# The embedding product of p_2 computed in the routing instead of in the feed-forward

## The chip, the cores and the metric

The kernel runs on one core of one Trainium2 chip. The metric is device time in microseconds (us) of one launch, as the median of several runs. The core has TensorE (PE, matmuls; PEld is its weight load), VectorE (DVE), ScalarE (ACT), GpSimd (POOL) and SyncE (SP, which only issues transfers here). Each engine works through a list of instructions of its own; the lists meet at semaphores.

## The reference

Two transformer blocks, one after the other, on x of 256 rows (tokens) by 1024 columns, all in float32. Cut to what matters here:

```python
# first block
x = x + concat([a_out, r_out]) @ w_out          # latent attention and retention
x = x + memory_cross_attention(rms_norm(x), rms_norm(mem), ...)
x = x + hierarchical_moe(rms_norm(x), ...)      # 4 groups of 8 experts: a router chooses for each token
                                                # one group, and two experts of that group
# second block
h = rmsnorm(x, g_mix);  z = h @ w_in            # recurrent and convolution heads
x = x + merged @ w_out
h = rmsnorm(x, g_ffn)
g, u = split(h @ w_gate_up)
x = x + (silu(g) * u) @ w_down                  # w_gate_up 1024 x 5632, w_down 2816 x 1024
gate = sigmoid(rmsnorm(x, g_ple) @ w_ple_gate)
x = x + gate * (p_i @ w_ple)                    # p_i = p_2, 256 x 256; w_ple 256 x 1024
return rmsnorm(x, g_final)
```

The product `p_i @ w_ple` depends on two inputs of the kernel alone, so it can be computed at any time before the last gate.

## The kernel before

Every float32 operand of a wide matmul is split in two parts of a shorter format: ACT copies the high part (names in `_hi`), DVE subtracts it from the source and keeps the low part (`_lo`), and PE adds three products (high by high, low by high, high by low: `three`, one line each in the profile, L2185 to L2187). Tokens lie in two tiles of 128 rows (t = 0, 1), columns in chunks of 512 (c = 0, 1); one matmul is 128 x 128 by 128 x 512 into one of eight PSUM banks.

Weights stream in units of 1 MB. SP loads unit u into one of three places of `stage` (in the expert part also into three places of `more`), ACT writes `w_hi` of it (L428 to L434), DVE `w_lo` (L441 to L449), PE uses it. `w_hi` and `w_lo` hold three units each: unit u takes the place of unit u - 3, so ACT waits for `unit_done` of that one, and SP's next load into a place of `stage` waits for `lo_ready`.

The order of the work is written out by hand, one list for each engine, in the places that the change touches as follows.

- **End of the cross attention.** PE multiplies by the four units of `cross_w_o` (`wide_unit` with U_CO to U_CO + 3). DVE in the meantime makes the low parts of the last units, runs a chain of tiny operations for the second block's decay (`lam_t`, `softplus2`, L1816 to L1827), the low part of the router's weights (`r_lo`), the low part of the first expert unit (U_MOE), and then `add_chunk(0, ...)`, L1739, which adds chunk 0 of the cross attention to x and signals `x_cross` = 1. After it come three constants (L1834 to L1836), the next unit and the low part of x. The second `add_chunk` signals `x_cross` = 2.
- **Routing.** PE transposes x for the router in two halves (`turn("moe", ...)`, L2190), the first on `x_cross` = 1, inside the last attention unit, the second on `x_cross` = 2. Then come 32 small products with the router's weights (L2506, L2508), the ranks of the tokens (L2515 to L2519) and, with DVE's `slot_of`, the gathering of the tokens for each expert (L2530, L2531). Between these stand 15 matmuls whose result nobody reads (`keep_busy`, L2490), 1 + 2 + 8 + 4.
- **Feed-forward of the second block.** 11 steps of 256 columns of the hidden layer. The columns of step 0 are computed first (`columns_of`, two units, 48 matmuls into banks 4 and 5); inside the second unit PE transposes p_2 (`turn_embed`); then `embed_product` computes `p_2 @ w_ple` with 24 matmuls into banks 0 to 3 from a weight unit of its own, U_PLE; ACT and DVE meanwhile turn step 0's columns into `hidden`. Then `turn_hidden(0)`, step 1 and so on. ACT copies the embedding product to `embed` (L1258).

Of the kernel before, what the change touches and what calls it, by code (L numbers as in the profile page):

```python
# [91 lines left out]
def program(nc, a, out, ctx):  # L92
# [78 lines left out]
    row_wide = xs[:, 1, 0:T * P].rearrange("p (t q) -> p t q", t=T)  # L171
    scale_row, scale_row2 = xs[:, 0, 0:256], xs[:, 0, 256:512]

# [65 lines left out]
    p_in = rb("p_in", [P, T, 256])  # L239
# [33 lines left out]
    embed, ple_gate = sb("embed", [P, T, D]), sb("ple_gate", [P, T, D])  # L273
# [35 lines left out]
    U_PLE = U_FFN + 2  # L309
    FFN_BASE = U_FFN + 1  # L310
# [7 lines left out]
    embed_unit = (a["w_ple_2"][0].rearrange("(p k) n -> p (k n)", k=2), 2048)  # L318
# [25 lines left out]
    main_pairs = swiglu_pairs(U_MOE, EXPERTS) | {U_FFN, FFN_BASE} | (swiglu_pairs(FFN_BASE, STEPS_FFN) - {FFN_BASE, FFN_BASE + 1})  # L344
# [35 lines left out]
    def slot_free(sp, st, u0):  # L380

        if st.last_in_slot(u0) is not None:
            sp.wait_ge(st.lo_ready, st.last_in_slot(u0) + 1)
        elif st is main and st.places[u0] >= RING:
            sp.wait_ge(sem("x_cross"), 1)

# [106 lines left out]
    def chunk_lo(dve, u0, c, st=main):  # L493
# [14 lines left out]
                + [f"mix{n}" for n in range(4)] + [("scales", 4)]  # L508
                + [("ffn0", 6), ("ffn1", 7), ("ffn2", 6), ("ffn3", 7), ("pT", 7), ("ple0", 4), ("ple1", 5), ("ple2", 6), ("ple3", 7)])
# [77 lines left out]

    def flat3(v):
        return v.rearrange("p k t -> p (k t)")
# [27 lines left out]
    def up_done(base, e):  # L617

        return base + 1 if isinstance(e, int) and e == 0 else e * 3 + (base + 1)
# [37 lines left out]

    def part_bank(k):

        return bank[k % 6]  # L660
# [126 lines left out]
    def _(sp):  # L787
# [16 lines left out]
        for u in range(3, U_MOE):  # L804
            load_unit(sp, *before[u], u)

        def swiglu_loads(both_of, down_of, base, steps, st=main, before_steps=None):
# [10 lines left out]
            if before_steps:  # L818
                before_steps(both)
            else:  # L820
                both(0, 0, base)
                both(0, 1, base + 1)
# [38 lines left out]
        def ffn_start(both):  # L861
            both(0, 0, U_FFN)
            both(0, 1, U_FFN + 1)
            load_unit(sp, *embed_unit, U_PLE)

        swiglu_loads(lambda c, half: [gu2[:, 4 * half:4 * half + 4, w, bass.ds(c * FF, FF)] for w in range(2)],
                     lambda c: down2[bass.ds(c, 1)].rearrange("c p n -> p (c n)"), FFN_BASE, STEPS_FFN,
                     before_steps=ffn_start)
# [11 lines left out]
    def _(pool):  # L880
# [10 lines left out]
        pool.wait_ge(sem("rx_hi"), 1)  # L891
# [6 lines left out]
    def _(act):  # L898
# [334 lines left out]
        warm_up(ACT.Exp)  # L1233
        act.wait_ge(sem("route_diffs"), 1)
        nc.scalar.activation(exps[:], diffs[:], ACT.Exp).then_inc(sem("route_exps"), 1)

        def swiglu(name, base, steps, scale_of):

            def tanhs(e):
                act.wait_ge(unit_done, up_done(base, e))  # L1240
                for t in range(T):
                    nc.scalar.activation(silu_t[:, t], bank[4 + t][:, 0:FF], ACT.Tanh, scale=scale_of(t)).then_inc(sem(name + "_tanh"), 1)
# [5 lines left out]
            def step(i, first=False):  # L1248
                if not first:
                    split_hi(act, SLOT, base + 1, 3, i)  # L1250
# [19 lines left out]
        def experts(name, st, base, groups, nth_tail, before_tail=None, splits=(None, None)):  # L1270

            for k in range(KD):
                act.wait_ge(sem(name + "_gathered"), k + 1)
# [4 lines left out]
                ins.then_inc(sem(name + "_xg_hi"), 1)  # L1278
# [1683 lines left out]
```

## Time and profile before

| | us |
|---|---|
| median of 3 runs | 960.63 |
| lowest and highest run | 958.66, 961.14 |
| span of the profiled execution, first to last instruction | 957.2 |
| PE busy in it | 941.8 (98%) |
| DVE busy | 743.1 (78%) |
| ACT busy | 621.3 (65%) |
| SP's transfers, share of 16 DMA engines | 63.2% |

The profiled execution has no time of its own beside its span; the median lies 3.43 us above the span, for what runs ahead of the first and behind the last instruction. A busy time of PE counts matmuls whose ends are modelled and overlap, so the starts of the matmuls, not their lengths, tell the pace. "Busy" does not tell either what PE does: the 15 matmuls of `keep_busy` count in it.

### The profile page before, as it was taken

The page shows a single profiled execution, that of the slowest core. Times are in us where ns is not written, and L with a number is a line of the kernel's source. Part 1 is how long each engine was busy: PE and PEld are TensorE (multiplying, and loading weights), DVE is VectorE, ACT ScalarE, POOL GpSimd, SP SyncE. Part 2 cuts the span into 40 slices and gives each one's busy share as a digit, 9 for nine tenths or more (in the row PEclk, how much of TensorE's full clock was granted, in tenths as well). Part 3 has the DMA queues.
Part 4 walks back from the last instruction along what each step waited for, and adds up shares of the span by engine and source line. Part 5 has one row for each costly group of instructions (what it writes and reads, how often), then busy time and mean ns, then how long its engine had stood idle before and what let it go on. Part 6 is the DMA issues. An engine that isn't in the chain of part 4 may idle for free.

```text
span 957.2 us, 13873 instructions
## 1 busy us (share of the span) xinstructions
PE 941.8 (98%) x5047; PEld 811.6 (85%) x5047; DVE 743.1 (78%) x1105; ACT 621.3 (65%) x946; POOL 20.5 (2%) x40
## 2 busy tenths in 40 slices
PE   8999999999999999999999999999999999999996
PEld 7888888888888888888888899999998888888885
DVE  6657696658799999999999889888896655555575
ACT  6785784665678878788787675757564644434455
POOL 2400000000000000000000000000000000000000
PEclk9999999999999999999999999999999999999998
DMA  9855336416299999999997364736465656555521
GB/s 340 239 182 180 132 94 214 164 58 250 95 372 372 343 367 369 355 365 370 358 372 271 111 225 126 255 120 210 152 234 183 220 179 204 186 177 182 199 102 44
DMA packets 102668, 214.68 MB, mean 224 GB/s; under 512 B 5644, under 2 KB 60192, under 8 KB 96992
## 3 DMA queue, kind: packets, MB, share of 16 engines
q1 hardware_dynamic: 100928, 211.57, 63.2%
q0 software_dynamic: 1392, 2.20, 0.9%
q8 instruction: 26, 0.43, 0.2%
q10 hardware_dynamic: 304, 0.33, 0.1%
q14 instruction: 18, 0.15, 0.0%
HBM read 213.03 MB, written 1.05 MB: 224 GB/s over the span
## 4 chain that ended last, share of the span: by engine, by line
PE 91%; DVE 4%; ACT 3%; issue 1%; DMA 1%; SPq 0%; DVEq 0%; ACTq 0%
PE bank L2185 22%; PE bank L2187 22%; PE bank L2186 22%; PE bank L2848 5%; PE bank L2849 5%; PE bank L2850 5%; PE bank L2190 4%; PE bank L2455 1%; DMA xs<-in_mem_dram 1%; DVE w_lo L449 1%; PE bank L2530 0%; PE bank L2531 0%; PE bank L2875 0%; PE bank L2876 0%; PE bank L2874 0%
## 5 line engine op out<-in xcount | busy, mean ns | idle before, releaser
L2185 PE MATMUL bank<-w_hi,xT_hi 128*128 128x512 f32 (+1 forms) x704 | 279.8, 397 | 0.6 <-DVE xT_lo L1522 0.3
L2187 PE MATMUL bank<-w_hi,xT_lo 128*128 128x512 f32 (+1 forms) x704 | 274.3, 390 | 0.0
L2186 PE MATMUL bank<-w_lo,xT_hi 128*128 128x512 f32 (+1 forms) x704 | 274.0, 389 | 0.0
L2185 PEld LDWEIGHTS bank<-w_hi,xT_hi 128*128 128x128 f32 x704 | 132.7, 189 | 27.3 <-issue 2.1
L2187 PEld LDWEIGHTS bank<-w_hi,xT_lo 128*128 128x128 f32 x704 | 132.1, 188 | 27.5
L2186 PEld LDWEIGHTS bank<-w_lo,xT_hi 128*128 128x128 f32 x704 | 132.4, 188 | 25.1
L447 DVE TENSOR_TENSOR w_lo<-stage,w_hi 128x1024 fp32r<-128x1024 f32 (+3 forms) x98 | 112.3, 1146 | 30.8 <-ACT w_hi L433 29.5
L2848 PE MATMUL bank<-xT_hi,w_hi 128*128 128x256 f32 x440 | 124.8, 284 | 0.4 <-DVE w_lo L449 0.4
L2849 PE MATMUL bank<-xT_lo,w_hi 128*128 128x256 f32 x440 | 124.5, 283 | 0.0
L2850 PE MATMUL bank<-xT_hi,w_lo 128*128 128x256 f32 x440 | 124.5, 283 | 0.0
L433 ACT ACTIVATE w_hi<-stage 128x1024 fp32r<-128x1024 f32 (+3 forms) x99 | 98.5, 995 | 31.8 <-PE bank L2187 14.5
L449 DVE TENSOR_TENSOR w_lo<-stage,w_hi 128x1024 fp32r<-128x1024 f32 (+3 forms) x98 | 111.9, 1142 | 0.0
L434 ACT ACTIVATE w_hi<-stage 128x1024 fp32r<-128x1024 f32 (+3 forms) x99 | 97.8, 988 | 0.0
L441 DVE TENSOR_TENSOR w_lo<-stage,w_hi 128x1024 fp32r<-128x1024 f32 x55 | 67.1, 1220 | 28.5 <-ACT w_hi L428 27.8
L428 ACT ACTIVATE w_hi<-stage 128x1024 fp32r<-128x1024 f32 x55 | 58.3, 1059 | 44.0 <-PE bank L2187 44.0
L2848 PEld LDWEIGHTS bank<-xT_hi,w_hi 128*128 128x128 f32 x440 | 84.4, 192 | 0.7 <-DVE w_lo L449 0.6
L2850 PEld LDWEIGHTS bank<-xT_hi,w_lo 128*128 128x128 f32 x440 | 84.4, 192 | 0.0
L2849 PEld LDWEIGHTS bank<-xT_lo,w_hi 128*128 128x128 f32 x440 | 84.4, 192 | 0.0
L2185 PE MATMUL bank<-w_hi,aT_hi 128*128 128x512 f32 x212 | 82.7, 390 | 0.1
L2187 PE MATMUL bank<-w_hi,aT_lo 128*128 128x512 f32 x212 | 82.8, 390 | 0.0
L2186 PE MATMUL bank<-w_lo,aT_hi 128*128 128x512 f32 x212 | 82.5, 389 | 0.0
L443 DVE TENSOR_TENSOR w_lo<-stage,w_hi 128x1024 fp32r<-128x1024 f32 x55 | 67.0, 1217 | 0.0
(425 smaller groups left out, 1384.0 us busy)
## 6 DMA issues: line engine op xcount, KB each, us to landing
stage<-in_w_in_dram SPq DMA_DIRECT2D x36, 1024.0 KB, 5.1
stage<-in_w_gate_up_dram SPq DMA_DIRECT2D x44, 512.0 KB, 4.6
more<-in_expert_w_down_dram SPq DMA_DIRECT2D x17, 1024.0 KB, 6.2
stage<-in_expert_w_gate_dram SPq DMA_DIRECT2D x33, 512.0 KB, 5.1
stage<-in_expert_w_up_dram SPq DMA_DIRECT2D x33, 512.0 KB, 6.3
more<-in_expert_w_gate_dram SPq DMA_DIRECT2D x31, 512.0 KB, 5.1
more<-in_expert_w_up_dram SPq DMA_DIRECT2D x31, 512.0 KB, 6.0
stage<-in_expert_w_down_dram SPq DMA_DIRECT2D x15, 1024.0 KB, 6.8
```

The costliest lines, as they stand in the source:

```text
L433: nc.scalar.activation(w_hi[:, s, 0:half], src[:, 0:half], ACT.Copy).then_inc(st.half_ready, 1)
L434: nc.scalar.activation(w_hi[:, s, half:cols], src[:, half:cols], ACT.Copy).then_inc(st.hi_ready, 1)
L441: nc.vector.tensor_tensor(beside(w_lo, s, 0), of_both(st, u0, 0), beside(w_hi, s, 0).bitcast(F32), ALU.subtract)
L443: nc.vector.tensor_tensor(beside(w_lo, s, 1), of_both(st, u0, 1), beside(w_hi, s, 1).bitcast(F32), ALU.subtract).then_inc(st.lo_ready, 1)
L447: nc.vector.tensor_tensor(w_lo[:, s, 0:half], src[:, 0:half], w_hi[:, s, 0:half].bitcast(F32), ALU.subtract)
L449: nc.vector.tensor_tensor(w_lo[:, s, half:cols], src[:, half:cols], w_hi[:, s, half:cols].bitcast(F32), ALU.subtract).then_inc(st.lo_ready, 1)
L2185: mm(o, k_hi, v_hi, start=start, stop=False)
L2186: mm(o, k_hi, v_lo, start=False, stop=False)
L2187: return mm(o, k_lo, v_hi, start=False, stop=stop)
L2848: mm(o, w_hi[:, s, at:at + P], xT_hi[:, k, :], start=k == 0, stop=False)
L2849: mm(o, w_hi[:, s, at:at + P], xT_lo[:, k, :], start=False, stop=False)
L2850: ins = mm(o, w_lo[:, s, at:at + P], xT_hi[:, k, :], start=False, stop=k == KD - 1)
```

## The change

`p_2 @ w_ple` moves from the feed-forward into the end of the cross attention and the routing.

- Weights and input: `w_ple` is loaded by SP behind the load of U_CO, into memory of its own (`ple_in`), and split by ACT (`ple_hi`) and DVE (`ple_lo`) there. The unit U_PLE is gone, so the feed-forward's units are numbered on without it. p_2 is loaded early, into `hidden`.
- PE transposes p_2 inside unit U_CO + 2 (before its second of four slices). ACT and DVE split the transposed tile (`aT_hi`, `aT_lo`) right behind the splitting of U_CO + 3.
- The 15 unread matmuls are gone. In their places stand the 24 matmuls of the product: 9 before the second half of the router's transposes, 9 behind the router's products, 6 behind the ranks. The router's 32 products now stand in one piece.
- ACT copies the product to `embed` before the routing's exponentials; `embed` takes the memory of `xs`, so results that nobody reads of the later squares go elsewhere.
- The gathering uses the banks in the order 4, 5, 2, 3, 0, 1 and waits for the copies of the embedding product in banks 2, 3, 0, 1.
- Feed-forward: step 0's columns go to banks 2 and 3, step 1's to 4 and 5, so both are computed back to back, and `turn_hidden(0)` stands between the two units of step 1.
- SP's first load into `more` also waits for `ple_lo`. The expert part and its second pass for overflowing groups, which is not run with this input, share semaphores.

```diff
@@ SP
         for u in range(3, U_MOE):
             load_unit(sp, *before[u], u)
+            if u == U_CO:
+                sp.wait_ge(sem("x_attn"), 1)
+                sp.dma_start(ple_in[:], a["w_ple_2"][0].rearrange("(p k) n -> p (k n)", k=2)).then_inc(sem("ple_loaded"), 16)
...
-            load_unit(sp, *embed_unit, U_PLE)
@@ ACT
         nc.scalar.activation(r_hi[:], r_w[:], ACT.Copy).then_inc(sem("router_hi"), 1)
+        act.wait_ge(sem("ple_loaded"), 16)
+        act.wait_ge(unit_done, U_CO + 1)
+        for n in range(2):
+            at = slice(1024 * n, 1024 * n + 1024)
+            nc.scalar.activation(ple_hi[:, at], ple_in[:, at], ACT.Copy).then_inc(sem("ple_hi"), 1)
         splits_to(U_CO + 4)
+        copy_to(aT_hi[:], "pT").then_inc(sem("pT_hi"), 1)
         warm_up(ACT.Sqrt)
         splits_to(U_MOE + 2)
...
         warm_up(ACT.Exp)
+        for n, (c, t) in enumerate(EMBED_ORDER):
+            act.wait_ge(sem("embed_filled"), n + 1)
+            nc.scalar.activation(embed[:, t, 512 * c:512 * c + 512], bank[2 * c + t][:, :], ACT.Copy).then_inc(sem("embed_copied"), 1)
         act.wait_ge(sem("route_diffs"), 1)
...
-                if first:
-                    for c in range(2):
-                        for t in range(T):
-                            nc.scalar.activation(embed[:, t, 512 * c:512 * c + 512], bank[2 * c + t][:, :],
-                                                 ACT.Copy).then_inc(sem("embed_copied"), 1)
@@ DVE
         low_parts("catc", None, (2, 3))
+        splits_to(U_CO + 3)
+        for n in range(2):
+            at = slice(1024 * n, 1024 * n + 1024)
+            dve.wait_ge(sem("ple_hi"), n + 1)
+            ins = tt(ple_lo[:, at], ple_in[:, at], ple_hi[:, at].bitcast(F32), ALU.subtract)
+        ins.then_inc(sem("ple_lo"), 1)
         splits_to(U_CO + 4)
+        dve.wait_ge(sem("pT_hi"), 1)
+        frees(tt(flat3(aT_lo[:]), bank[where["pT"][0]][:, :], flat3(aT_hi[:]).bitcast(F32), ALU.subtract), "pT")
@@ PE
-        wide_unit(U_CO + 2, C_CO, 1, 512, xT_hi, xT_lo, "catc")
+        wide_unit(U_CO + 2, C_CO, 1, 512, xT_hi, xT_lo, "catc", before={1: turn_embed})
...
-        for half in range(2):
-            if half == 0:
-                b = to_fill(pe, "router")
...
-                if k == 2:
-                    turn("moe", x, [("x_cross", 2)], (2, 3))
-                if k % 4 == 0:
-                    keep_busy(1 + half)
...
+        been_read(pe, "pT")
+        pe.wait_ge(sem("ple_lo"), 1)
+        embed_product([(0, 0), (0, 1), (1, 0)])
+        turn("moe", x, [("x_cross", 2)], (2, 3))
+        b = to_fill(pe, "router")
...
-        keep_busy(8)
+        embed_product([(1, 1), (2, 0), (2, 1)])
         pe.wait_ge(sem("group_chosen"), 1)
...
-        keep_busy(4)
+        embed_product([(3, 0), (3, 1)])
...
                 for k in range(6):
+                    if t == 0 and k >= 2:
+                        pe.wait_ge(sem("embed_copied"), k - 1)
                     ins = gather(k, t)
...
             columns_of(0, U_FFN, 0, 0, before={2: lambda: turn("ffn", x, [("x_rnn", 2)], (2, 3))})
-            columns_of(1, U_FFN + 1, 0, 0, before={3: turn_embed})
-            embed_product()
-            turn_hidden(0)
+            columns_of(1, U_FFN + 1, 0, 0)
...
-                pe.wait_ge(sem(name + "_hidden"), i * 2)
+                if not first:
+                    pe.wait_ge(sem(name + "_hidden"), i * 2)
                 columns_of(0, base - 1, 3, i)
+                if first:
+                    turn_hidden(0)
                 columns_of(1, base, 3, i)
@@ new functions on PE
+        def embed_product(blocks):
+            for n, k in blocks:
+                c, t = EMBED_ORDER[n]
+                at = D * k + 512 * c
+                ins = three(bank[2 * c + t][:, :], aT_hi[:, k, P * t:P * t + P], aT_lo[:, k, P * t:P * t + P],
+                            ple_hi[:, at:at + 512], ple_lo[:, at:at + 512], start=k == 0, stop=k == 1)
+                if k == 1:
+                    ins.then_inc(sem("embed_filled"), 1)
+    EMBED_ORDER = ((1, 0), (1, 1), (0, 0), (0, 1))
+    def columns_bank(e, t):
+        return bank[(2 if isinstance(e, int) and e == 0 else 4) + t]
```

DVE at the end of the cross attention, from the low parts of U_CO + 3 to the addition that signals `x_cross` = 1 (`w_lo<-stage` is the splitting of a weight unit, `ple_lo` that of w_ple, `lam_t` the first link of the chain of tiny operations, `r_parts` the router's weights), before:

```order
L1530 TENSOR_TENSOR xT_lo<-bank,xT_hi 128x512 x2
L447 TENSOR_TENSOR w_lo<-stage,w_hi 128x1024
L449 TENSOR_TENSOR w_lo<-stage,w_hi 128x1024
L1816 TENSOR_SCALAR lam_t<-lam_t 128x8
...
L1827 TENSOR_SCALAR lam_t<-softplus 128x8
L1829 TENSOR_TENSOR r_parts<-r_w,r_parts 128x8x36
...
L441 TENSOR_TENSOR w_lo<-stage,w_hi 128x4x256
L443 TENSOR_TENSOR w_lo<-stage,w_hi 128x4x256
L1739 TENSOR_TENSOR x<-x,bank 128x512 x2
```

and now:

```order
L1539 TENSOR_TENSOR xT_lo<-bank,xT_hi 128x512 x2
L1825 TENSOR_TENSOR ple_lo<-ple_in,ple_hi 128x1024 x2
L451 TENSOR_TENSOR w_lo<-stage,w_hi 128x1024
L453 TENSOR_TENSOR w_lo<-stage,w_hi 128x1024
L1829 TENSOR_TENSOR aT_lo<-bank,aT_hi 128x512
L1833 TENSOR_SCALAR lam_t<-lam_t 128x8
...
L1844 TENSOR_SCALAR lam_t<-softplus 128x8
L1846 TENSOR_TENSOR r_parts<-r_w,r_parts 128x8x36
...
L445 TENSOR_TENSOR w_lo<-stage,w_hi 128x4x256
L447 TENSOR_TENSOR w_lo<-stage,w_hi 128x4x256
L1748 TENSOR_TENSOR x<-x,bank 128x512 x2
```

Two splittings of w_ple stand ahead of U_CO + 3, and the splitting of the transposed p_2 (`aT_lo`) ahead of the chain; what follows is in the order that it had.

PE from the last transposes of x in the attention to the gathering (`r_parts` 128x72 and 128x36 are the router's products, 16 in each half before, `hot` the ranks, `slot_of` the gathering), before:

```order
L2190 MATMUL bank<-const,x 128x128 x8
...
L2495 MATMUL bank<-zeros,before_it 128x144
L2490 MATMUL bank<-r_parts,before_it 128x512
L2506 MATMUL bank<-r_parts,xT_hi 128x72
L2508 MATMUL bank<-r_parts,xT_lo 128x36
...
L2190 MATMUL bank<-const,x 128x128 x8
...
L2490 MATMUL bank<-r_parts,before_it 128x512 x2
...
L2490 MATMUL bank<-r_parts,before_it 128x512 x8
L2515 MATMUL bank<-hot,before_it 128x4
...
L2490 MATMUL bank<-r_parts,before_it 128x512 x4
L2530 MATMUL bank<-slot_of,xs_hi 128x512
```

and now:

```order
L2206 MATMUL bank<-const,x 128x128 x8
...
L2201 MATMUL bank<-ple_hi,aT_hi 128x512
L2202 MATMUL bank<-ple_lo,aT_hi 128x512
L2203 MATMUL bank<-ple_hi,aT_lo 128x512
...
L2206 MATMUL bank<-const,x 128x128 x8
L2527 MATMUL bank<-zeros,before_it 128x144
L2534 MATMUL bank<-r_parts,xT_hi 128x72
L2536 MATMUL bank<-r_parts,xT_lo 128x36
...
L2543 MATMUL bank<-hot,before_it 128x4
...
L2557 MATMUL bank<-slot_of,xs_hi 128x512
```

The unread products with `before_it` and `r_parts` of 512 columns are gone; the first of the triplets with `ple_hi` stand ahead of the second transposes of x (9 matmuls), further ones between the router's products and the ranks (9) and between the ranks and the gathering (6).

PE at the start of the feed-forward (`p_in` is p_2, `xT_hi` are columns of a step, `aT_hi` with `w_hi` the embedding product), before:

```order
L2187 MATMUL bank<-w_hi,xT_lo 128x512
L2190 MATMUL bank<-const,p_in 128x128 x4
L2185 MATMUL bank<-w_hi,xT_hi 128x512
...
L2185 MATMUL bank<-w_hi,aT_hi 128x512
...
L2190 MATMUL bank<-const,hidden 128x128 x4
L2185 MATMUL bank<-w_hi,xT_hi 128x512
```

and now:

```order
L2203 MATMUL bank<-w_hi,xT_lo 128x512
L2206 MATMUL bank<-const,hidden 128x128 x4
L2201 MATMUL bank<-w_hi,xT_hi 128x512
L2202 MATMUL bank<-w_lo,xT_hi 128x512
L2203 MATMUL bank<-w_hi,xT_lo 128x512
```

The columns of step 0 and the first unit of step 1 run on into each other, and the transposes of `hidden` follow on these.

## Rows read from the trace of the kernel before

**Rows 1.** The page: engine busy times, and the chain that ended last by engine.

```profile
PE 941.8 (98%) x5047; PEld 811.6 (85%) x5047; DVE 743.1 (78%) x1105; ACT 621.3 (65%) x946; POOL 20.5 (2%) x40
...
PE 91%; DVE 4%; ACT 3%; issue 1%; DMA 1%; SPq 0%; DVEq 0%; ACTq 0%
```

**Rows 2.** Chain that ended last, in order, 215 to 256: start us, us, what.

```profile
223.46 1.28 DVE x L1739 x2
...
230.15 1.20 DVE x L1739 x2
...
239.97 0.61 PE bank L2530
```

**Rows 3.** Timeline of DVE: start us, us, instruction, count, idle time before and releaser.

```profile
213.73 1.23 DVE L447 TENSOR_TENSOR w_lo<-stage,w_hi 128x1024 fp32r<-128x1024 f32 x1 [1.04 <-ACT w_hi L433]
...
216.01 0.17 DVE L1816 TENSOR_SCALAR lam_t<-lam_t 128x8 f32<-128x8 f32 x1
...
220.19 1.23 DVE L441 TENSOR_TENSOR w_lo<-stage,w_hi 128x1024 fp32r<-128x1024 f32 x1
...
223.46 1.28 DVE L1739 TENSOR_TENSOR x<-x,bank 128x512 f32<-128x512 f32 x2 [0.91 <-PE bank L2187]
...
224.66 0.22 DVE L1834 TENSOR_SCALAR ones<-const 128x128 fp32r<-128x128 f32 x1
```

**Rows 4.** Timeline of ACT, end of the cross attention.

```profile
212.64 1.06 ACT L433 ACTIVATE w_hi<-stage 128x1024 fp32r<-128x1024 f32 x1
```

**Rows 5.** Timeline of PE, end of the cross attention and routing.

```profile
217.82 0.39 PE L2185 MATMUL bank<-w_hi,xT_hi 128*128 128x512 f32 x1
...
227.34 1.03 PE L2190 MATMUL bank<-const,x 128*128 128x128 f32 x8
...
231.40 1.09 PE L2190 MATMUL bank<-const,x 128*128 128x128 f32 x8
...
235.77 2.09 PE L2490 MATMUL bank<-r_parts,before_it 128*128 128x512 f32 x8
...
239.97 0.61 PE L2530 MATMUL bank<-slot_of,xs_hi 128*128 128x512 f32 x1 [0.17 <-issue]
...
246.22 0.63 PE L2530 MATMUL bank<-slot_of,xs_hi 128*128 128x512 f32 x1
```

**Rows 6.** Windows: stretch, us, busy us of PE, PEld, DVE, ACT, POOL, clock, DMA, GB/s.

```profile
170.00:212.00 42.00, 41.56 (x211) 35.21 (x210) 24.12 (x47) 25.69 (x56) 0.00 (x0) 1.00 0.37 125
...
223.46:229.60 6.14, 6.14 (x33) 5.14 (x31) 6.10 (x12) 5.24 (x10) 0.00 (x0) 1.00 0.54 185
...
229.60:239.97 10.37, 9.68 (x63) 7.65 (x61) 8.66 (x28) 5.12 (x11) 0.00 (x0) 1.00 0.99 390
...
239.97:252.85 12.88, 12.87 (x61) 12.03 (x61) 9.97 (x52) 6.17 (x17) 0.00 (x0) 1.00 0.02 6
...
950.50:951.00 0.50, 0.00 (x0) 0.00 (x0) 0.47 (x2) 0.46 (x3) 0.00 (x0) 0.70 0.00 0
```

**Rows 7.** Timeline of PE, start of the feed-forward.

```profile
742.10 0.63 PE L2190 MATMUL bank<-const,p_in 128*128 128x128 f32 x4
...
744.21 0.50 PE L2185 MATMUL bank<-w_hi,aT_hi 128*128 128x512 f32 x1
...
749.81 0.63 PE L2190 MATMUL bank<-const,hidden 128*128 128x128 f32 x4
```

**Rows 8.** Timeline of ACT and DVE, start of the feed-forward.

```profile
742.76 0.60 ACT L975 ACTIVATE aT_hi<-bank 128x512 fp32r<-128x512 f32 x1 [2.61 <-PE bank L2190]
...
743.46 0.69 DVE L2124 TENSOR_TENSOR aT_lo<-bank,aT_hi 128x512 fp32r<-128x512 f32 x1 [1.79 <-ACT aT_hi L975]
...
745.27 1.28 ACT L1242 ACT_TABLE_LOAD   x1
...
747.08 0.79 DVE L1873 SCALAR_TENSOR_TENSOR silu_g<-silu_t,bank 128x256 f32<-128x256 f32 x2 [0.37 <-ACT silu_t L1242]
...
750.97 1.57 ACT L1258 ACTIVATE embed<-bank 128x512 f32<-128x512 f32 x3
```

More of the change, by code:

```diff
@@ L270, in program @@
     expert_memory.close()
-    embed, ple_gate = sb("embed", [P, T, D]), sb("ple_gate", [P, T, D])
+    routing_memory = ExitStack()
+    routing_memory.enter_context(nc.sbuf_tensor("before_embed", [P, 5120], F32))
+    ple_hi, ple_lo = (routing_memory.enter_context(nc.sbuf_tensor(n, [P, SLOT], F32R)) for n in ("ple_hi", "ple_lo"))
+    routing_memory.enter_context(nc.sbuf_tensor("between_embed", [P, 896], F32))
+    ple_in = routing_memory.enter_context(nc.sbuf_tensor("ple_in", [P, SLOT], F32))
+    routing_memory.close()
+    embed, p_in = xs, hidden
+    ple_gate = sb("ple_gate", [P, T, D])
     fin_g = sb("fin_g", [P, D])
@@ L816, in step @@
                 load_unit(sp, down_of(i), 2048, base + n + 4, st=st)
[L818 to L822, printed above, removed]
+            both(0, 0, base)
+            both(0, 1, base + 1)
             for i in range(steps - 1):
@@ L2116, in _ @@
         add_chunk(1, C_OUT2, U_OUT2 + 3, "x_rnn")
-        stats(x, xs, [("x_rnn", 2)], "ffn")
+        stats(x, ple_gate, [("x_rnn", 2)], "ffn")
         low_parts("ffn", FFN_G, (2, 3))
         halves("ffn")
-        splits_to(U_PLE + 1)
         dve.wait_ge(sem("norm_half"), NORMS.index("ffn") + 1)
         then(tt(ffn_scale[:], half_rstd[:], rstd[:], ALU.mult))
-        dve.wait_ge(sem("pT_hi"), 1)
-        frees(tt(flat3(aT_lo[:]), bank[where["pT"][0]][:, :], flat3(aT_hi[:]).bitcast(F32), ALU.subtract), "pT")
         swiglu("ffn", FFN_BASE, STEPS_FFN, lambda t, e: ffn_scale[:, t:t + 1])
@@ L2412, in _, with turn_embed @@
         wide_unit(U_CQ + 2, C_CQ, 1, 512, xT_hi, xT_lo, "crossq")
+        def turn_embed():
+            pe.wait_ge(sem("last_loaded"), 16)
+            b = to_fill(pe, "pT")
+            view = p_in[:].rearrange("p t (q k) -> p t k q", k=2)
+            for k in range(2):
+                for t in range(T):
+                    ins = transpose(b[:, 256 * k + P * t:256 * k + P * t + P], view[:, t, k])
+            fills(ins, "pT")
+        def embed_product(blocks):
[6 more added lines that the diff above has]
+                    ins.then_inc(sem("embed_filled"), 1)
         def turn_queries(p):
@@ L2897, in _ @@
                           last=(lambda: turn("ffn", x, [("x_rnn", 1)], (0, 1))) if half and c else None)
-        def turn_embed():
-            pe.wait_ge(sem("last_loaded"), 32)
-            b = to_fill(pe, "pT")
-            view = p_in[:].rearrange("p t (q k) -> p t k q", k=2)
-            for k in range(2):
-                for t in range(T):
-                    ins = transpose(b[:, 256 * k + P * t:256 * k + P * t + P], view[:, t, k])
-            fills(ins, "pT")
-        def embed_product():
-            been_read(pe, "pT")
-            pe.wait_ge(lo_ready, U_PLE + 1)
-            s = U_PLE % RING
-            for c in range(2):
-                for k in range(2):
-                    for t in range(T):
-                        at = D * k + 512 * c
-                        ins = three(bank[2 * c + t][:, :], aT_hi[:, k, P * t:P * t + P], aT_lo[:, k, P * t:P * t + P],
-                                    w_hi[:, s, at:at + 512], w_lo[:, s, at:at + 512], start=k == 0, stop=k == 1)
-            ins.then_inc(unit_done, 1)
         swiglu("ffn", FFN_BASE, STEPS_FFN)
```

164 lines of the change are left out of this document (76 added, 88 removed), and 2 rows, old and new, of the table products.

## The prediction

> **What bounds the kernel now.** I read the page first: PE is busy 98% of the span and 91% of the chain that ended last is PE's [rows 1]. So a matmul taken off PE is worth its time, unless another engine decides at that place. The places where the change works are two, and I read each for itself.
>
> In the feed-forward PE starts a matmul every 0.23 us without a pause, so it is the bound there. The embedding product runs from 744.21 to 749.81 [rows 7].
>
> In the routing the busy share misleads, because 15 matmuls there are read by nobody. The view to read is the chain in order of time: at 223.46 it is on DVE (the addition of chunk 0 to x), at 230.15 again (the addition of chunk 1), and for the gathering it is back on PE at 239.97 [rows 2]. DVE is busy 6.10 of the 6.14 us from 223.46 to 229.60, where PE leaves the attention [rows 6], and the only idle time that it had shortly before is 0.91 us in front of the addition at 223.46, waiting for PE [rows 3]. So whatever comes to DVE before 223.46 beyond 0.91 us moves the routing.
>
> **The feed-forward: what PE saves.** Removed are the four transposes of p_2, which start at 742.10, and the product. The matmuls' pace: from 217.82, the start of a unit, to 227.34 stand 24 + 18 = 42 matmuls [rows 5], 9.52 / 42 = 0.227 us each. Six matmuls follow the transposes in their unit, and the product starts at 744.21. So transposes, six matmuls and the wait for the split p_2 take 744.21 - 742.10 = 2.11 us, of which the six matmuls are 1.36; 0.75 goes. Of that about 0.46 are the transposes and 0.25 the wait. The product is 749.81 - 744.21 = 5.60 us [rows 7]. Together 6.35 us.
>
> What is late next is step 1. Its first unit needs no result of step 0 and can follow at once: its splitting now stands where U_PLE's stood, ahead of 742. `turn_hidden(0)` needs `hidden`, which DVE has some 3 us after the end of step 0's columns (before: end of the columns at 744.0, then `aT_hi` and a unit's copy on ACT, table load at 745.27, DVE's gating at 747.08 [rows 8]); the 24 matmuls in between give 5.4 us of cover. The second unit of step 1 must be split behind the tanh: ACT's table load can start at 743.6 instead of 745.27, so DVE's gating comes at about 745.4 and the low part 3.9 us later, at 749.3; PE wants it at 743.5 + 5.45 + 0.4 = 749.35. I charge 0.1 us; the end of 0.6 us holds if ACT and DVE each lose 0.25 more. The embedding copies on ACT, some 0.5 us each (three of them in 1.57 us [rows 8]), leave this place and hid nothing. The loads are one less. Feed-forward: -6.25 us, between -6.35 and -5.75.
>
> **The end of the cross attention: what DVE gets.** Everything here is of forms that the trace shows.
>
> PE: the four transposes of p_2 stand behind six matmuls of unit U_CO + 2, which starts at 217.82: 217.82 + 6 x 0.227 = 219.18. They cost PE 0.46 us as before.
>
> ACT: the two copies of w_ple come first, at 212.64 where the unit U_CO + 3 was copied [rows 4], which moves to about 214.6 to 216.6. Then ACT waits for the transposes. Before, ACT's `aT_hi` started 0.66 us and DVE's `aT_lo` 1.36 us behind the start of the transposes (742.10, 742.76, 743.46), and DVE was free about 0.61 us later [rows 7, 8]. So `aT_hi` at 219.84, `aT_lo` at 220.54, DVE free at 221.15. Behind `aT_hi` ACT has a table load, 1.28 us as in [rows 8], and U_MOE's copy, from 221.85 on.
>
> DVE: at 213.73 stands the low part of U_CO + 3, two instructions 1.14 us apart, then the chain from 216.01 [rows 3]. Now `ple_lo` takes 213.73 to 216.01, U_CO + 3 to 218.29, and then DVE waits 2.25 us for `aT_hi`. Queued behind the waiting instruction are the chain of tiny operations (216.01 to 220.19, 4.18 us), U_MOE (220.19 to 222.47) and the addition at 223.46 that PE's transposes wait for [rows 3]. From 221.15 they end at 227.61. The addition is late by 227.61 - 223.46 = 4.15 us: 2.28 of `ple_lo`, 0.61 of `aT_lo`, 2.25 of waiting, less 0.99 of slack (the 0.91 and what lies between).
>
> All of this is passed on. PE reaches the transposes at 227.34 + 0.46 = 227.80 and waits 1.1 us for `x_cross` = 1. DVE goes on late by 4.15 without slack to the second addition, at 234.30. PE has then finished the unit and the first 9 matmuls of the product by about 233.4 and waits some 2.2 us. PE's 0.46 us and these 9 matmuls are free in this.
>
> The Trainium skill, "TensorE: Matmul & The Clock Gate", section on the array's architecture, says that ACT and DVE take their instructions in strict order, only PE pulling weight loads ahead; this speaks against putting a wait in front of the chain. The trace agrees: the constant `ones` needs nothing that is late, yet DVE idled 0.91 us at 223.46 with it queued and did it at 224.66 [rows 3]. Could DVE pass the waiting instruction, the chain would fill the 2.25 us and the sum would come out at -4.1 us instead of -1.9.
>
> **The routing itself.** Before, the second transposes start at 231.40, directly on `x_cross` = 2, and the gathering at 239.97, 8.57 us later [rows 5]. Now: the router's 32 products stand in one piece behind them; that costs about 0.2 us, since the first 16 no longer run before. The 9 product matmuls behind (2.04 us) replace the 8 unread ones that start at 235.77 and last 2.09 us, to 237.86 [rows 5]; that was just ahead of the ranks, so this is covered to 0.1 us. The 6 behind the ranks replace 4: 2 x 0.227 = 0.45 more, of which about 0.2 was idle (0.17 before 239.97). So the gathering starts later by 0.35 us beside the 4.15. DVE allowed its seventh pair only at 246.22 [rows 5], about 0.15 us after PE could have gone on, so 0.2 stays. The copies to `embed` on ACT, 0.5 each, end ahead of the last bank's turn, which comes 2.5 us into the gathering. I take +0.2 us; the ends are 0 and 0.8 (nothing hidden: 0.2 + 0.45 + a wait on the last copy). The load of w_ple is one unit among SP's others at a place where the queues are 37% busy (170 to 212 [rows 6]), 40 us ahead of its use; zero. `more` is loaded 4.2 us later with the rest, and the queues were at 2% from 239.97 to 252.85 [rows 6], so the experts do not wait: zero, at most 0.3.
>
> **Sum.** -6.25 + 4.15 + 0.2 = -1.9 us. The span goes from 957.2 to 955.3, and with the 3.43 us between span and median the median goes from 960.63 to **958.7 us**. The addition's 4.15 is uncertain by 0.7 either way (start of the transposes, semaphore times); with the bounds above the case's own range is 957.5 to 960.1.
>
> **Rivals.**
>
> *The lateness is absorbed.* Then only PE's own part counts: -6.25 + 0.46 + 0.2 = -5.6, 955.0 us. It needs DVE's wait for `aT_hi` and the `ple_lo` work to lie in slack that I did not see, for example an addition that is not what the routing turns on. Against it stands the chain, which has DVE without a gap there [rows 2], and DVE's busy time of 6.10 in 6.14 us [rows 6]. Half of it (2 us of lateness less) gives 956.8. Chance 0.16 for both.
>
> *The clock falls.* The only place of the trace where the granted clock fell, from 1.00 to 0.50 with 0.70 as the mean of the half microsecond between (950.50 to 951.00 [rows 6]), is about 2.3 us behind the last matmul, which ended at 948.36. The new pauses are 1.1 and 2.2 us, and the second is followed by transposes and matmuls of 36 to 72 columns until about 240, where 1 + 2 full ones stood before. If the clock goes to 1.2 GHz there, a full matmul costs twice 0.227: 15 of the product's add 3.4 us, behind which DVE's ranks and the gathering wait, and about 7 gathering matmuls 1.7 more. +5.1 us: 963.8 us, slower than now. It is slower than now from 1.9 us on, that is, from 8 full matmuls at the low level; against it speaks that the pause is a little shorter than the one at the end, and that the clock held at 1.00 through 229.60 to 239.97 with 0.7 us idle and many small matmuls [rows 6]. Chance 0.20.
>
> *The change doesn't shorten the feed-forward.* If step 1's second unit came late by the whole splitting (2.3 us) instead of 0.1, the sum would be +0.3, 960.9 us. ACT starting 1.7 us earlier speaks against it. It counts as part of "no change", chance 0.04.
>
> **Numbers.** Forecast 0.60, absorbed 0.16, clock 0.20, late unit 0.04. A difference of 0.3% is 2.9 us, about what a measurement of this kernel tells from no change; it lies at 957.7 and 963.5. Faster: the absorbed cases 0.14 of 0.16 and the forecast's lower tail, 0.08: 0.22. Slower: most of the clock's case and a bit else: 0.18. The same: 0.60. The range for 8 in 10 leaves out about half of each rival: 955.4 to 963.5 us.
>
> **What the profile would show.** DVE's addition to x after U_CO + 2 at about 227.6 instead of 223.46, with an idle time of 2.2 us in front of `aT_lo`; two waits of PE for the additions, 1.1 and 2.2 us; the gathering at 244.3; in the feed-forward the matmuls of step 0 and of step 1's first unit without a gap, `turn_hidden(0)` 5.4 us behind the end of step 0's columns, and no triplets with `aT_hi` between them; granted clock 1.00 through the routing. Wrong would be: an addition at 225 or earlier, no pause of PE before the second transposes, a clock under 1.00 in the routing, or a wait of PE for `w_lo` at the second unit of step 1.

## The result, and the profile after

The changed kernel takes 962.86 us (median of 5 runs, 959.74 to 964.21), the kernel before, beside it, 959.66 us (5 runs, 958.66 to 961.14). The ratio is 1.0029 with the interval [1.0019, 1.0040]: slower by some 2.8 us (the medians differ by 3.2), where 1.9 us less was forecast. The profiled execution took 962.86 us with a span of 961.1 us, 3.9 us more than the 957.2 of before.

The page after, in the lines that answer to [rows 1]:

```profile
PE 943.4 (98%) x5032; PEld 813.8 (85%) x5032; DVE 743.3 (77%) x1105; ACT 621.6 (65%) x946; POOL 20.5 (2%) x40
...
PE 91%; DVE 5%; ACT 2%; issue 1%; DMA 1%; SPq 0%; DVEq 0%; ACTq 0%
```

PE has 15 matmuls less (the unread ones; the product and its transposes have only moved) and is yet busy for 1.6 us longer. A busy time that grows with fewer instructions says that some of them became slower.

DVE's timeline after, against [rows 3] (start, us, instruction, idle time before and releaser):

```profile
220.37 0.69 DVE L1829 TENSOR_TENSOR aT_lo<-bank,aT_hi 128x512 fp32r<-128x512 f32 x1 [2.12 <-ACT aT_hi L979]
...
227.44 1.28 DVE L1748 TENSOR_TENSOR x<-x,bank 128x512 f32<-128x512 f32 x2
...
234.05 1.28 DVE L1748 TENSOR_TENSOR x<-x,bank 128x512 f32<-128x512 f32 x2
...
242.26 0.23 DVE L711 COPY biased<-bank 128x72 f32<-128x72 f32 x1 [3.11 <-PE bank L2536]
...
247.07 0.17 DVE L724 SCALAR_TENSOR_TENSOR hot_rank<-bank,hot 128x8 f32<-128x8 f32 x1 [2.26 <-PE bank L2547]
```

Down to the second addition this is the forecast: the wait for `aT_hi`, the addition at 227.44 instead of 223.46. The last two rows are not. DVE waits 3.11 us for the router's products and 2.26 us for the ranks, both PE's; the bound of this stretch has passed from DVE to PE.

PE's timeline after, against [rows 5]:

```profile
228.77 1.09 PE L2206 MATMUL bank<-const,x 128*128 128x128 f32 x8 [0.88 <-DVE x L1748]
...
232.97 0.40 PE L2203 MATMUL bank<-ple_hi,aT_lo 128*128 128x512 f32 x1
235.38 1.09 PE L2206 MATMUL bank<-const,x 128*128 128x128 f32 x8 [2.01 <-DVE x L1748]
...
241.77 0.38 PE L2536 MATMUL bank<-r_parts,xT_lo 128*128 128x36 f32 x1
241.99 0.77 PE L2201 MATMUL bank<-ple_hi,aT_hi 128*128 128x512 f32 x1
242.56 0.63 PE L2202 MATMUL bank<-ple_lo,aT_hi 128*128 128x512 f32 x1
242.99 0.63 PE L2203 MATMUL bank<-ple_hi,aT_lo 128*128 128x512 f32 x1
...
246.89 0.77 PE L2201 MATMUL bank<-ple_hi,aT_hi 128*128 128x512 f32 x1
...
249.60 0.63 PE L2557 MATMUL bank<-slot_of,xs_hi 128*128 128x512 f32 x1
```

The pauses of 0.88 and 2.01 us are the forecast's 1.1 and 2.2. But the product's matmuls start 0.43 us apart (242.56, 242.99), where the full matmuls of the kernel before stood 0.227 us apart at 217.82 to 227.34. Windows of the changed kernel, against [rows 6] (stretch, us, busy us of PE, PEld, DVE, ACT, POOL, granted clock, DMA, GB/s):

```profile
237.00:237.50 0.50, 0.50 (x7) 0.50 (x6) 0.49 (x2) 0.50 (x2) 0.00 (x0) 1.00 0.86 295
237.50:238.00 0.50, 0.50 (x6) 0.50 (x5) 0.50 (x2) 0.14 (x1) 0.00 (x0) 0.64 0.93 246
238.00:250.50 12.50, 12.50 (x43) 10.88 (x43) 6.64 (x27) 5.23 (x9) 0.00 (x0) 0.50 0.49 193
...
251.00:251.50 0.50, 0.50 (x3) 0.41 (x2) 0.45 (x2) 0.22 (x1) 0.00 (x0) 0.70 0.00 0
251.50:253.00 1.50, 1.50 (x8) 1.50 (x8) 1.26 (x8) 0.00 (x0) 0.00 (x0) 1.00 0.04 11
```

The granted clock is the share of TensorE's full 2.4 GHz that it ran at. From about 237.6 to 251.2 us it stands at 0.50, the level of 1.2 GHz, though PE is busy without a gap. Ahead of the fall lie the 2.01 us of waiting, eight transposes and some ten products of 36 and 72 columns.

The feed-forward, against [rows 7 and 8], two rows of the kernel before first:

```profile
729.03 1.03 PE L2190 MATMUL bank<-const,x 128*128 128x128 f32 x8
...
766.64 0.63 PE L2190 MATMUL bank<-const,hidden 128*128 128x128 f32 x4
```

and after:

```profile
738.86 1.03 PE L2206 MATMUL bank<-const,x 128*128 128x128 f32 x8
...
758.72 0.63 PE L2206 MATMUL bank<-const,hidden 128*128 128x128 f32 x4
...
770.11 0.63 PE L2206 MATMUL bank<-const,hidden 128*128 128x128 f32 x4
```

The turn of x that ends the recurrent block starts 9.8 us later than before (729.03), but the turn of step 1's `hidden` only 3.5 us later (before 766.64): 31.25 us lie between the two instead of 37.61, so 6.36 us are saved. With 0.4 us that the last stage is longer this is the whole difference of the two spans: 9.83 - 6.36 + 0.4 = 3.9 us.

### The profile page after: what moved, and what is told of

The parts are those of the page before. It is cut to its first block, busy times and chain, and to the rows that moved or that the text cites. A ratio compares the mean times of both kernels' runs of the same rounds, so it can differ in the third digit from the quotient of the medians.

```text
span 961.1 us, 13854 instructions
## 1 busy us (share of the span) xinstructions
PE 943.4 (98%) x5032; PEld 813.8 (85%) x5032; DVE 743.3 (77%) x1105; ACT 621.6 (65%) x946; POOL 20.5 (2%) x40
## 4 chain that ended last, share of the span: by engine, by line
PE 91%; DVE 5%; ACT 2%; issue 1%; DMA 1%; SPq 0%; DVEq 0%; ACTq 0%
PE bank L2201 22%; PE bank L2203 22%; PE bank L2202 22%; PE bank L2876 5%; PE bank L2877 5%; PE bank L2878 5%; PE bank L2206 4%; PE bank L2490 1%; DMA xs<-in_mem_dram 1%; DVE w_lo L453 0%; PE bank L2558 0%; PE bank L2557 0%; DVE w_lo L445 0%; PE bank L2903 0%; PE bank L2904 0%
## 5 line engine op out<-in xcount | busy, mean ns | idle before, releaser
L451 DVE TENSOR_TENSOR w_lo<-stage,w_hi 128x1024 fp32r<-128x1024 f32 (+3 forms) x97 | 111.1, 1145 | 27.3 <-ACT w_hi L437 26.1
L437 ACT ACTIVATE w_hi<-stage 128x1024 fp32r<-128x1024 f32 (+3 forms) x98 | 97.4, 994 | 32.5 <-PE bank L2203 14.5
L453 DVE TENSOR_TENSOR w_lo<-stage,w_hi 128x1024 fp32r<-128x1024 f32 (+3 forms) x97 | 110.8, 1142 | 0.0
L438 ACT ACTIVATE w_hi<-stage 128x1024 fp32r<-128x1024 f32 (+3 forms) x98 | 96.8, 988 | 0.0
L2203 PE MATMUL bank<-w_hi,aT_lo 128*128 128x512 f32 x204 | 79.6, 390 | 0.0
L2201 PE MATMUL bank<-w_hi,aT_hi 128*128 128x512 f32 x204 | 79.5, 389 | 0.0
L2202 PE MATMUL bank<-w_lo,aT_hi 128*128 128x512 f32 x204 | 79.4, 389 | 0.0
```

Source lines behind the costliest of these rows:

```text
L437: nc.scalar.activation(w_hi[:, s, 0:half], src[:, 0:half], ACT.Copy).then_inc(st.half_ready, 1)
L438: nc.scalar.activation(w_hi[:, s, half:cols], src[:, half:cols], ACT.Copy).then_inc(st.hi_ready, 1)
L451: nc.vector.tensor_tensor(w_lo[:, s, 0:half], src[:, 0:half], w_hi[:, s, 0:half].bitcast(F32), ALU.subtract)
L453: nc.vector.tensor_tensor(w_lo[:, s, half:cols], src[:, half:cols], w_hi[:, s, half:cols].bitcast(F32), ALU.subtract).then_inc(st.lo_ready, 1)
L2201: mm(o, k_hi, v_hi, start=start, stop=False)
L2202: mm(o, k_hi, v_lo, start=False, stop=False)
```

## The experiments

Theory 1 is that the lost clock turned the small gain into a loss. Theory 2 is that DVE's lateness and the new order did. Twelve kernels ran in three groups of four, each group beside the kernel before (959.1 to 959.3 us). A mean clock is the granted clock averaged over a whole run; the kernel before has 0.995 to 0.998. Some code lines are shortened.

**1. Unread matmuls in PE's second pause.**

```diff
         embed_product([(0, 0), (0, 1), (1, 0)])
+        for _ in range(8):
+            mm(bank[6][:, :], before_it[:], r_parts 512 columns, start=True, stop=True)
         turn("moe", x, [("x_cross", 2)], (2, 3))
```

> The changed kernel with eight unread 128x512 matmuls (8 x 0.227 = 1.82 us at the full clock) put into TensorE's wait of 2.01 us in front of the transposes at 235.4 us. Theory 1, the lost clock is what made the change slower: the granted clock stays at 1.00 from 236 to 251 us, the router's pitch is 0.107 instead of 0.213 us, the MoE's first columns start some 5 us earlier than in the changed kernel (near 253 instead of 258 us), and the time is about 0.998 of the kernel before (957.5 to 958.5 us). Theory 2, VectorE's late addition and the new order cost the time and the clock only goes along with it: the clock may stay up, but VectorE's and ScalarE's chain ends where it ended, and the time stays within 1 us of the changed kernel's, 1.002 to 1.004 of before. Theory 3, the clock isn't kept by matmuls in that pause (it falls for what is in the router's small products): the granted clock is 0.50 from about 238 us all the same, and the time is 1.003 of before or a little over it.

Measured: 958.35 us, ratio 0.9996 [0.9985, 1.0007], 12 runs: the median is 0.8 us under that of the kernel before, where the changed kernel's was 3.2 us over it. The interval takes in no difference, so this is a loss undone, not a gain. The nine runs with a mean clock of 0.995 or more have a median of 957.7 us. The profiled run had a span of 956.1 us. Its windows (PE alone: stretch, us, busy us, granted clock, DMA, GB/s), then DVE's first addition and PE's timeline:

```profile
232.00:235.00 3.00, 3.00 (x14) 1.00 0.80 284
235.00:238.00 3.00, 2.85 (x25) 1.00 0.99 348
238.00:241.00 3.00, 3.00 (x25) 1.00 1.02 365
```

```profile
227.61 1.28 DVE L1748 TENSOR_TENSOR x<-x,bank 128x512 f32<-128x512 f32 x2
...
235.55 1.09 PE L2206 MATMUL bank<-const,x 128*128 128x128 f32 x8 [0.15 <-DVE x L1748]
...
239.97 0.26 PE L2538 MATMUL bank<-r_parts,xT_lo 128*128 128x36 f32 x1
240.09 0.48 PE L2201 MATMUL bank<-ple_hi,aT_hi 128*128 128x512 f32 x1
...
244.42 0.46 PE L2559 MATMUL bank<-slot_of,xs_hi 128*128 128x512 f32 x1
```

DVE's second addition stands where it stood (234.22; 234.05 in the changed kernel), and with the clock at 1.00 the gathering starts at 244.42 instead of 249.60; the forecast had 244.3. Theory 1 holds, and theory 2 falls: DVE's lateness is still there, and the loss is gone. Not every run kept the clock: the eight at 957.1 to 958.9 us have a mean clock of 0.995 to 0.998 and the one at 959.2 us has 0.996, but the one at 960.1 us has 0.994, and the two at 961.6 and 962.2 us have 0.993.

**2. The kernel before without its unread matmuls** (`keep_busy` issues none).

> The kernel before with its 15 unread matmuls in the routing left out, nothing else. It prices the clock without the change's other parts. Theory 1: the granted clock falls to 0.50 in the routing, somewhere in 230 to 240 us, the gathering starts and ends 3 to 5 us later, and the time is 1.003 to 1.005 of before (962.5 to 964.5 us). Theory 2: within 0.1% of before, since the routing is set by VectorE's and ScalarE's chain, and the gathering alone pays for a lower clock (under 1 us).

Measured: 961.5 us, ratio 1.0028 [1.0017, 1.0039], the mean clock 0.991 to 0.993 in all 7 runs. The router's pitch doubles at 234.3 us, without any pause over 0.67 us before it:

```profile
232.00:234.00 2.00, 1.33 (x14) 1.00 1.00 322
234.00:236.00 2.00, 2.00 (x13) 0.59 0.98 338
```

```profile
239.09 0.38 PE L2515 MATMUL bank<-hot,before_it 128*128 128x4 f32 x1 [2.11 <-DVE hot L690]
```

So it is these 15 matmuls that kept the clock in the kernel before. The time stood just below what I expected (1.003 to 1.005). A likely reason, not tested by itself: here PE still waits 2.11 us for DVE's group choice, and what stands in such a wait costs nothing at the low clock. In the changed kernel 15 matmuls at this place are work that the ranks and the gathering wait for.

**3. The lambda chain early.** ACT's `Abs` and `Exp` and DVE's 18 small operations are moved ahead of the split of `catc` (2, 3).

> The changed kernel with the chain for lambda (two activations, 18 small VectorE operations, 2.3 us) moved ahead of the split of cross attention's last parts, into VectorE's idle time before 212 us. VectorE's addition that turns out the MoE's columns then comes 1.5 to 2.5 us earlier than in the changed kernel (near 225.5 instead of 227.4 us). Theory 1: TensorE's pauses shift and their sum changes little, so the clock falls as before, and only the 1.5 to 2.5 us come back: 0.9995 to 1.001 of before (959.5 to 961 us); if the clock should hold, 954.5 to 956 us. Theory 2: the time comes back by the whole of the lateness removed, with the clock at 0.50 or not, to about 1.000.

Measured: 956.37 us, ratio 0.9978 [0.9966, 0.9991]. The addition starts at 225.32, 2.1 us earlier, and PE's second pause is 1.02 us. The profiled run kept the clock through the router, which ends at 237.80, and lost it at about 238.3, in the full matmuls of the product, for some 3.4 us (PE alone):

```profile
237.00:238.00 1.00, 1.00 (x10) 1.00 1.00 393
238.00:239.00 1.00, 1.00 (x4) 0.68 1.04 426
239.00:240.00 1.00, 1.00 (x3) 0.50 1.08 447
```

Its runs are two groups: five at 955.1 to 956.5 us (0.995 to 0.997), three at 958.4 to 959.3 us (0.991 to 0.993). The median lies between the two ranges that I had given for a lost and a kept clock. From 3.2 us over the kernel before it has come to 2.75 us under it: 2.1 us are the addition's, and the rest I put down to a fall that comes later or, by the mean clocks, perhaps not at all; one profile can't tell how the others went.

**4. The feed-forward alone.** The routing is that of the kernel before. The embedding product, the splits of w_ple_2 and the transposes of p_2 are left out, and eight of the 15 unread matmuls write the product's banks, so the kernel is incomplete.

> The feed-forward of the changed kernel with the routing of the kernel before: the embedding product, its transposes and the splits of w_ple_2 and p_2 are left out everywhere, and eight of the unread matmuls of before write the banks of the product instead, so that the gated embedding is computed from other values. It prices the feed-forward's part alone: by the prediction's own sum -6.25 us, 953.0 to 954.0 us, 0.9935 of before, with the clock at 1.00 in the routing. A rival, that the feed-forward gave back less than the trace seems to show (a late second unit, a slower clock there), would be 0.996 or more.

Measured: 952.5 us, ratio 0.9938 [0.9925, 0.9951]; just under the 953.0 to 954.0 that I expected; the span is 950.6, 6.6 us less than before, with the clock at 1.00 in the routing. From the turn of x to the turn of step 1's `hidden` it is 31.24 us, 6.37 less than before and as in the changed kernel. The first term stands.

**5 and 6. Early order, with and without unread matmuls.** Beside run 3's edit:

```diff
         splits_to(U_CO + 4)                      # ScalarE
-        copy_to(aT_hi[:], "pT")
         warm_up(ACT.Sqrt)
+        splits_to(U_MOE + 1)
+        copy_to(aT_hi[:], "pT")
...
         splits_to(U_MOE + 1)                     # VectorE
+        aT_lo <- pT, aT_hi
         add_chunk(0, C_CO, U_CO + 2, "x_cross")
```

Run 5 has four unread matmuls ahead of the second transposes too, and two in the middle of the router's product.

> The changed kernel with the lambda chain moved early as in the third run, the splits of p_2's transposes (ScalarE and VectorE) moved behind the split of the MoE's first unit, four unread 128x512 matmuls in front of the second transposes and two in the middle of the router's product. If the two losses (VectorE's lateness of 4.1 us, and the clock) are what took the gain, VectorE's addition comes within 0.7 us of where it stood before (223.5 us), the clock stays at 1.00 from 223 to 256 us, and the time is 0.993 to 0.996 of before (952.5 to 955.5 us). If something else in the routing costs as well (the order in which TensorE does product and router), it is 0.997 or more with both cured.

> As the run beside it, without the six unread matmuls. The clock theory: with the pauses shortened only, the router's 32 small matmuls remain, the clock falls in the profile or in a part of the runs (mean granted clock of a run 0.993 or lower beside 0.997), and such runs are 2 to 4 us longer: a median of 953.5 to 957.5 us, in two groups. The rival (the clock falls only for a pause over 1.1 us without work): it holds in every run, and the median is 0.5 us under that of the run beside it, since six matmuls are saved.

Measured: run 5 956.2 us, 0.9966 [0.9955, 0.9978], the clock at 0.995 or more in all six runs; run 6 954.13 us, 0.9943 [0.9930, 0.9955], five runs at 953.5 to 955.2 and one at 958.3 us (0.991). The addition is at 223.93 and 224.21. Run 5 missed its range (0.993 to 0.996). Its second transposes start at 233.09 instead of 231.40: 9 product and 4 unread matmuls, all of them now on PE's path, stand where PE used to do half of the router. Here the unread matmuls are not free, as nothing else is waited for.

The profile of run 6 happened on a run in which the clock fell, and it is the most telling one:

```profile
232.21 0.40 PE L2204 MATMUL bank<-ple_hi,aT_lo 128*128 128x512 f32 x1
232.45 1.04 PE L2207 MATMUL bank<-const,x 128*128 128x128 f32 x8
```

```profile
232.00:234.00 2.00, 2.00 (x18) 1.00 0.97 342
234.00:236.00 2.00, 2.00 (x20) 1.00 0.94 291
236.00:238.00 2.00, 2.00 (x12) 0.62 1.01 397
238.00:240.00 2.00, 2.00 (x6) 0.50 1.06 444
```

The fall is at 236.4, where the products' pitch doubles. PE is busy in every microsecond from 200 us up to it, and the transposes wait for nothing. A pause isn't needed; eight transposes and 28 products of 36 and 72 columns in a row came before it.

**7 and 8. Where the unread matmuls must stand.** The changed kernel with eight in the pause and two in the middle of the router (7), and with eight in the middle of the router alone (8).

> The changed kernel with eight unread matmuls in the pause, as in the first run, and two more in the middle of the router's product (0.45 us on TensorE's way to the router's result). If the runs of the first experiment at 960 to 962 us were ones in which the clock fell, they are gone here: every run within 1 us of the median, mean granted clock 0.996 or more in each, median 957.3 to 958.3 us, 0.998 to 0.9995 of before. If their spread has another cause, runs at 960 us and above appear here too, at a clock of 0.997.

> The changed kernel with eight unread matmuls in the middle of the router's product and none in the pause. It tells the pause from the small products. If it is the pause of 2.0 us that makes the clock fall, it falls all the same, near 237.5 us, before or in those eight, and the time is 1.003 to 1.005 of before. If it is the long stretch of small products, the clock holds, at the price of 8 x 0.227 = 1.8 us in front of the router's result: 1.000 to 1.002 of before (959 to 961 us).

Measured: run 7 958.68 us, 0.9992 [0.9983, 1.0000], eleven runs between 957.5 and 959.3 us, for 0.45 us more work. The runs above 960 us, 3 of 12 in run 1, do not appear, but so few could be missing by chance. The median is above the 957.3 to 958.3 that I expected, and four runs have a mean clock of 0.994 or 0.995 instead of 0.996 or more. Run 8: 963.13 us, 1.0062 [1.0038, 1.0085], over the range for a fall too: four runs at 962.7 to 963.2 us with 0.994, two at 968.5 and 969.2 us with 0.986 and 0.987. In its profile the clock falls ahead of the eight, which then run slowly themselves (PE alone):

```profile
235.00:238.00 3.00, 2.52 (x16) 0.70 1.02 343
238.00:241.00 3.00, 3.00 (x13) 0.50 0.97 328
```

With the pause left open, filling what follows is too late to prevent the fall. Of the two slowest runs there is no profile, and why they are 5 us longer is open.

**9 to 12. Real work as the filler, and controls.** Run 9 is run 6 with the third block of the product moved into the router's middle; run 10 is run 6 again; run 11 is the kernel before with only the first three of its unread matmuls; run 12 is the changed kernel again.

> The early variant without unread matmuls (sixth run), with the third block of the product (3 full matmuls of work that must be done anyway) moved from the front of the second transposes into the middle of the router's product. The clock theory, in the form that the runs so far leave (the router's 32 small products in a row bring the clock down, even without a pause): the clock holds now in every run (mean 0.995 or more), the second transposes start some 0.4 us earlier, the router's result comes within 0.3 us of the sixth run's at the full clock, and the median is 953.5 to 954.8 us, 0.994 to 0.9955 of before, without the runs at 958 us. The rival (the fall in the sixth run was chance, independent of the order): the same share of runs, 1 in 6, lies near 958 us.

> The sixth run's kernel again, beside its variant on one chip, for more runs: two groups, most at 953.5 to 954.5 us (granted clock 0.996 to 0.998) and some at 957 to 959 us (0.991), by the clock theory; by the rival, that 958.3 us was an outlier, one group.

> The kernel before with only three of its 15 unread matmuls, those in front of the router's first half (1) and in its middle (2). If it is the stretch of small products in the router that lowers the clock, three full matmuls beside them hold it up to the router's end, and it falls behind it at most, in VectorE's 4 us of group choice without work for TensorE: 1.000 to 1.002 of before (959 to 961 us). If any quiet of the whole stretch counts alike, it falls as with none: 1.0028 (961.5 us).

> The changed kernel itself once more, on the chip of these runs. The clock theory: most runs near 962.9 us at a mean granted clock of 0.988 to 0.991, and those in which the clock is 0.993 or more lie at 958 to 960 us. Else the clock and the time of a run don't go together.

Measured: run 9 955.26 us, 0.9959 [0.9946, 0.9972]; run 10 955.85 us, 0.9962 [0.9950, 0.9974]. Both have one run at 958.3 to 958.4 us with 0.991, and both profiles show 0.50 at 238 to 240 us. Two windows of run 9 beside it (PE alone):

```profile
236.00:238.00 2.00, 2.00 (x14) 0.81 1.00 397
...
240.00:242.00 2.00, 2.00 (x11) 0.84 0.56 238
```

Three full matmuls among the router's products do not keep the clock; my expectation of run 9 failed. But the fall came late in both profiles: in run 9 at 237.2, with the first full matmul behind the router, and it was over at 240.6; in run 10 at 238.0, in the fourth. So full matmuls don't stop a fall at once. Run 10 is no two clean groups either, but a slope: 954.2 us at 0.997, 956.5 at 0.993, 958.3 at 0.991. Run 11: 960.69 us, 1.0013 [1.0004, 1.0022], as expected: 1.00 to the end of the router at 235.4 us, then the fall in DVE's group choice (PE alone):

```profile
234.00:236.00 2.00, 1.61 (x15) 1.00 1.00 367
236.00:238.00 2.00, 0.28 (x2) 0.64 1.06 436
238.00:240.00 2.00, 0.94 (x5) 0.50 0.88 371
```

Run 12, 961.94 us, 1.0029 [1.0016, 1.0041], twelve runs: 964.4 to 964.9 us at a mean clock of 0.987 to 0.988, 961.8 to 962.6 at 0.990 to 0.991, 959.7 to 961.6 at 0.993 (the last beyond the 958 to 960 that I expected of these). Time and clock go together, and the fall comes at different moments (in this profile at 236.0, within the second transposes, in the first at 237.6). None of the 17 runs of the changed kernel has a mean clock over 0.993.

The kernel of run 6 is the fastest complete version: 954.1 us, or 955.9 us when repeated, 5.0 and 3.4 us under the kernel before. Run 9, beside the repeat, can't be told from it.

## Why the prediction was wrong

**The feed-forward, -6.25: right.** Measured -6.36, by the same two parts; step 1's second unit waits for nothing. The rival of the late unit is out, and run 4 gives the same 6.37 by itself.

**DVE's lateness, +4.15: right.** In run 1, which has the changed kernel's order and the clock of the kernel before, the addition is at 227.61. That this is the forecast to the hundredth is chance: the changed kernel, with the same instructions up to there, has 227.44. The rival that it is absorbed is out: PE waits for both additions, and in run 1, at the full clock, the gathering is 4.45 us late.

**The routing itself, +0.2: right.** The first turn of `hidden` in the MoE, before and in run 1:

```profile
257.73 0.50 PE L2190 MATMUL bank<-const,hidden 128*128 128x128 f32 x2
```

```profile
262.07 0.50 PE L2206 MATMUL bank<-const,hidden 128*128 128x128 f32 x2
```

It is 4.34 us later: 4.15 and 0.19.

**The sum, -1.9, as long as the clock holds: nearly.** Run 1's profiled span is 1.1 us under that of before. Its routing and feed-forward give 4.34 - 6.36 = -2.0 as forecast; 0.66 us are lost in the recurrent block, whose length is 197.76 instead of 197.10 us, the rest mostly in the last stage. The forecast had nothing for this block. Of the 0.66, 0.39 are one wait of PE that the kernel before doesn't have. It goes back to a weight load that landed late: ACT idled 3.46 us for it, where before it idled 1.33. Before, and then run 1:

```profile
569.59 1.06 ACT L433 ACTIVATE w_hi<-stage 128x1024 fp32r<-128x1024 f32 x1 [1.33 <-DMA stage<-in_w_in_dram]
```

```profile
576.11 1.06 ACT L437 ACTIVATE w_hi<-stage 128x1024 fp32r<-128x1024 f32 x1 [3.46 <-DMA stage<-in_w_in_dram]
...
589.10 0.39 PE L2878 MATMUL bank<-xT_hi,w_hi 128*128 128x256 f32 x1 [0.39 <-DVE w_lo L453]
```

The profiles of runs 5, 7 and 8 have the same two waits and 198.02, 198.23 and 197.90 us; all others have 197.1. These four are just the kernels that add unread matmuls to the changed one, so 0.7 to 1.1 us of their times seems to go with the filler itself. How it makes this load late is open.

**The clock: here it failed.** The step that failed is the forecast's "granted clock 1.00 through the routing": it put a lost clock at nothing in the sum and left it to the rival "the clock falls" with a chance of 0.20. The runs show 5.2 us for it at the gathering, which is late by 9.63 us in the changed kernel and by 4.45 in run 1. The measured 962.86 us lies inside the stated range only because that reached halfway into this rival. The rival had the mechanism right. Its size, 5.1 us, was near by luck, since its parts were off both ways: the 15 product matmuls cost 2.9 us (not 3.4), the router's products 2.0 and the ranks 0.3, which I had not charged, and the gathering 0.2 (not 1.7), as the clock was back after four of its matmuls. Up to the gathering I had 3.4 us and the runs show 5.2.

Both arguments against the fall were faulty. "The pause is shorter than the one at the end of the kernel" took the pause for the cause, and run 6 shows the fall without any. "The clock held through 229.60 to 239.97 with many small matmuls" was true, but of a stretch that held all 15 unread full ones as well; without them it does not hold (run 2). I had noted that these 15 matmuls are read by nobody and did not ask what they are for. The change put full matmuls back ahead of the second transposes and behind the router, but none into the router, and opened a pause of 2 us ahead of both.

Shown is that the fall costs about 5 us in the profiled runs (run 1 against the changed kernel; 4 us by the distances of the medians from the kernel before, as both kernels' runs differ) and that full matmuls in the pause prevent it in most runs (runs 1, 7), ones behind it don't (run 8). What exactly decides whether and when it comes is open: run 9 kept three full matmuls inside the router and lost the clock, run 5, with six, did not, and in the profiles of runs 3, 9 and 10 it fell only when full matmuls were running again.

## What to carry to other kernels

Work that nothing reads may be there for a reason, as here: before it is replaced, compare what PE does in each microsecond before and after, not how many matmuls there are. Put real work into a pause only if it also covers the stretch that the filler covered, and price the whole stretch at the low clock, small products included, because real work there is waited for where filler was not. And an operation that waits on another engine goes behind what doesn't need it: moving the lambda chain and `aT_lo` brought the kernel of runs 6 and 10 to 5.0 and 3.4 us under the kernel before, where run 1, the change with its clock mostly kept, has 0.8.

## What the runs showed of the hardware

The granted clock fell to 0.50 though PE was busy in all of the 4.00 us from 232 to 236 ahead of it (run 6), and it stayed there for 13.6 us in the changed kernel, 12.5 us of them busy without a gap in the windows above, before it rose. The products of 36 and 72 columns slow down as the full ones do: a pair took 0.22 us at 1.00 and 0.43 at 0.50. The clock can also fall while full matmuls run: in run 3 at 238.3, half a microsecond after they had started at 237.80. The same program falls at different moments from run to run (236.0 and 237.6 in the two profiles of the changed kernel), and its times spread over 5 us (959.7 to 964.9), in step with the mean clock, where the kernel before spreads over 1.5 (958.8 to 960.4).
